# A streaming encoder layer on one Trainium2 core: a tile's final sum kept in PSUM, and the router's logits computed in two column halves

## What is computed

```python
def route(h, w_router, router_bias):
    scores = jax.nn.sigmoid(jnp.matmul(h, w_router, preferred_element_type=jnp.float32))   # (1088, 64)
    biased = scores + router_bias.astype(jnp.float32)
    ...                                      # best 4 of 8 groups, best 8 experts in them, their weights

    ffn = swiglu(hf, w_sh_gate, w_sh_up, w_sh_down) + routed_experts(hf, top_idx, top_w, ...)
    x = x + g2 * ffn.reshape(b, t, d)
...
y_prompt = rms_norm(yp) * final_gain
y_sample = rms_norm(ys) * final_gain
```

## Time and profile before

| | us |
|---|---|
| median of 3 runs | 2242.13 (2235.76 to 2243.9) |
| the profiled execution | 2241.32 |
| its span | 2239.5 |
| `mix_and_route`, mix of tile 0 to the last logits | 1017.8 to 1157.0 |
| closing part, from PE's last expert matmul | 2162.8 to 2239.5 |
| PE busy | 2141.2 (96%) |
| DVE busy | 1237.4 (55%) |
| ACT busy | 1008.1 (45%) |
| POOL busy | 463.4 (21%) |

### The profile page before, as it was taken

How to read it: one execution, slowest core, us unless ns; L and a number is a source line. 1 busy time by engine, 2 the same in 40 slices (tenths; PEclk the granted TensorE clock), 3 DMA queues, 4 the chain that set the end, 5 groups by cost and what they waited for, 6 DMA issues and landing times. The chain is left out here.

```text
span 2239.5 us, 41417 instructions
## 1 busy us (share of the span) xinstructions
PE 2141.2 (96%) x11538; PEld 1835.2 (82%) x11539; DVE 1237.4 (55%) x2000; ACT 1008.1 (45%) x1773; POOL 463.4 (21%) x549
## 2 busy tenths in 40 slices
PE   5999899999999999999988999999999999999995
PEld 3767559999999999997868888888888888888862
DVE  3623683112232332216777787687677778668637
ACT  3403793211111121113432677677677677667622
POOL 2400000000000000000000444434443444434344
PEclk8999899999999999999998999999999999999998
DMA  7370501112111101116312999899889899989876
GB/s 295 113 254 9 177 1 57 38 47 66 48 47 44 31 19 47 47 66 230 116 55 87 309 318 321 248 314 328 269 289 340 279 322 306 318 250 322 261 220 157
DMA packets 153532, 395.59 MB, mean 177 GB/s; under 512 B 22124, under 2 KB 90932, under 8 KB 128900
## 3 DMA queue, kind: packets, MB, share of 16 engines
q1 hardware_dynamic: 122260, 311.61, 38.5%
q0 software_dynamic: 31040, 82.51, 15.1%
q10 hardware_dynamic: 176, 0.75, 0.1%
HBM read 353.93 MB, written 74.53 MB: 191 GB/s over the span
## 5 line engine op out<-in xcount | busy, mean ns | idle before, releaser
L2093 PE MATMUL ex_pgu<-ex_wgu_hi,ex_xT_hi 128*128 (+1 forms) x784 | 314.9, 402 | 9.5 <-DVE ex_xT_lo L2263 8.7
L2251 DVE TENSOR_TENSOR ex_wgu_lo<-ex_stage_gu,ex_wgu_hi (+1 forms) x252 | 291.8, 1220 | 37.3 <-ACT ex_wgu_hi L2170 37.3
L2093 PE MATMUL ex_pgu<-ex_wgu_hi,ex_xT_lo 128*128 (+1 forms) x784 | 308.0, 393 | 0.0
L2093 PE MATMUL ex_pgu<-ex_wgu_lo,ex_xT_hi 128*128 (+1 forms) x784 | 307.1, 392 | 0.0
L2170 ACT CAST ex_wgu_hi<-ex_stage_gu (+1 forms) x252 | 245.7, 1047 | 35.6 <-issue 16.3
L986 PE MATMUL cv_ph<-fourth_r,cv_split 128*128 128x352 f32 (+1 forms) x1152 | 221.8, 327 | 0.8 <-ACT cv_split L997 0.8
L986 PEld LDWEIGHTS cv_ph<-fourth_r,cv_split 128*128 128x128 f32 x1152 | 195.8, 188 | 1.0 <-ACT cv_split L997 1.0
L1627 POOL MEMSET ex_rows<- 128x1088 f32 x1 | 1.0, 1005 | 944.3 <-ACT third_r L1599 944.3
L2093 PEld LDWEIGHTS ex_pgu<-ex_wgu_hi,ex_xT_hi 128*128 128x128 f32 x784 | 148.4, 189 | 41.4 <-issue 11.5
L2093 PEld LDWEIGHTS ex_pgu<-ex_wgu_hi,ex_xT_lo 128*128 128x128 f32 x784 | 147.5, 188 | 31.4
L2093 PEld LDWEIGHTS ex_pgu<-ex_wgu_lo,ex_xT_hi 128*128 128x128 f32 x784 | 147.9, 189 | 28.6
(11 more groups left out here) (355 smaller groups left out, 4197.0 us busy)
## 6 DMA issues: line engine op xcount, KB each, us to landing
ex_stage_gu<-in_w_exp_gate SPq DMA_DIRECT2D x64, 1024.0 KB, 9.0
ex_stage_gu<-in_w_exp_up SPq DMA_DIRECT2D x64, 1024.0 KB, 11.6
ex_stage_dn<-in_w_exp_down SPq DMA_DIRECT2D x64, 1024.0 KB, 8.6
front_room<-in_w_ada SPq DMA_DIRECT2D x26, 512.0 KB, 5.9
w_ahead<-in_w_in SPq DMA_DIRECT2D x24, 512.0 KB, 3.8
third<-in_w_ada SPq DMA_DIRECT2D x16, 512.0 KB, 8.8
early_late<-in_w_in SPq DMA_DIRECT2D x16, 512.0 KB, 3.9
front_room<-in_w_in SPq DMA_DIRECT2D x3, 2048.0 KB, 12.5
```

The lines of the kernel that those rows point to most:

```text
L2093: last = pe.matmul(pgu[:, :], xT[a][:, k, :], w, start=(k == 0 and (a, c) == PASSES[0]), stop=(k == KT - 1 and (a, c) == PASSES[-1]))
L2251: dve.tensor_tensor(gu_piece(1, slot, q), gu_raw(slot, q), gu_piece(0, slot, q).bitcast(F32), ALU.subtract).then_inc(gu_lo, 1)
```

## The change

1. Closing part. The addition of a tile writes into its PSUM pair, no longer into `sums[t]`. Square (ACT) and the scaled output (DVE) read that pair. For this the banks are also declared as four pairs of 1024 columns (`x3_rows`), and the order in which banks are handed out is changed so that each pair lies side by side. PE's wait before it uses a pair again is now on `o_ready` (output t-4 made) in place of `x3` (addition t-4 done).
2. Router logits. The eight matmuls have 64 columns of `wr` stationary and the tile's up to 128 tokens moving; the first four blocks of the contraction go to PSUM partitions 0 to 63, the last four to 64 to 127, by turns. ACT copies this 128 x 128 result to SBUF (`halves_out`), at the beginning of its next round, and a matmul with a fixed 128 x 64 matrix (two identities, one above the other, `both_halves`, made once by DVE) adds the halves and brings them to the old place (`sum_halves`). It stands six rounds into `mix` of tile t+3, and for the last tiles behind `logits(7)` and four matmul records into `unit(0)` and `unit(1)`.

```diff
@@ mix_and_route
+            both_halves = room(NE)
+            halves = [room(P), little(P)]
...
+                            if (k, pw, px) == ROUNDS[5] and t >= 3:
+                                sum_halves(t - 3)
...
-                        for k in range(KT):
-                            last = pe.matmul(pl[t % 2][:R, 0:NE], h2T[:, k, t * P:t * P + R], wr[:, k, :],
-                                             start=(k == 0), stop=(k == KT - 1))
-                        last.then_inc(lg, 1)
+                        for k in range(KT // 2):
+                            for a in range(2):
+                                j = a * (KT // 2) + k
+                                last = pe.matmul(pl[t % 2][a * NE:(a + 1) * NE, P:P + R], wr[:, j, :], h2T[:, j, t * P:t * P + R],
+                                                 start=(k == 0), stop=(k == KT // 2 - 1))
+                        last.then_inc(lg_halves, 1)
+
+                    def sum_halves(t):
+
+                        R = rows_of(t)
+                        pe.wait_ge(sum_ready, 1)
+                        pe.wait_ge(lg_out, t + 1)
+                        pe.matmul(pl[t % 2][:R, 0:NE], halves[t % 2][:, 0:R], both_halves, start=True, stop=True).then_inc(lg, 1)
...
+                                if half == 0 and k == 1 and q < 2:
+                                    sum_halves(NT - 2 + q)
...
                     logits(NT - 2)
+                    sum_halves(NT - 3)
                     unit(0)
...
+                    def halves_out(t):
+                        R = rows_of(t)
+                        act.wait_ge(lg_halves, t + 1)
+                        act.copy(halves[t % 2][:, 0:R], pl[t % 2][:, P:P + R]).then_inc(lg_out, 1)
...
                     for t in range(NT):
                         R = rows_of(t)
+                        if t >= 2:
+                            halves_out(t - 2)
                         act.wait_ge(x2_done, t + 1)
...
+                    halves_out(NT - 2)
                     sigmoid(NT - 2)
...
                     evac(NT - 1)
+                    halves_out(NT - 1)
                     sigmoid(NT - 1)
...
+                    dve.tensor_tensor(both_halves, con[:, C_ID:C_ID + NE], con[:, C_ID + NE:C_ID + P], ALU.add).then_inc(sum_ready, 1)
@@ experts
+            with ExitStack() as pairs:
+                x3_rows = [pairs.enter_context(nc.psum_tensor(f"cb_x3_{i}", [P, D], F32)) for i in range(4)]
             pt = [ps(f"ex_pt{i}", [P, 4, P]) for i in range(2)]
             pgu = ps("ex_pgu", [P, 2 * DE])
+            ph_bank = ps("ex_ph", [P, 512])
+            for j in range(2):
+                ps(f"cb_p{j}", [P, 512])
             py = [ps(f"ex_py{j}", [P, 512]) for j in range(2)]
-            ph_bank = ps("ex_ph", [P, 512])
...
-            ptail = [ps(f"cb_p{j}", [P, 512]) for j in range(2)]
...
+            psum = [[v[:, j * 512:(j + 1) * 512] for j in range(2)] for v in x3_rows]
...
                         if t >= 4:
-                            pe.wait_ge(x3, t - 3)
+                            pe.wait_ge(o_ready, t - 3)
...
-                        link(act.activation(junk[:R, :], sums[t][:R, :], ACT.Square, accum_out=ss[:R, t:t + 1]))
+                        link(act.activation(junk[:R, :], x3_rows[t % 4][:R, :], ACT.Square, accum_out=ss[:R, t:t + 1]))
...
-                        dve.scalar_tensor_tensor(out_rows[:R, t % 3, :], sums[t][:R, :], ri[:R, t:t + 1], gain[:R, :],
+                        dve.scalar_tensor_tensor(out_rows[:R, t % 3, :], x3_rows[t % 4][:R, :], ri[:R, t:t + 1], gain[:R, :],
                                                  ALU.mult, ALU.mult).then_inc(o_ready, 1)
...
                         for j in range(2):
-                            last = dve.tensor_tensor(v[:, j * 512:(j + 1) * 512], v[:, j * 512:(j + 1) * 512], psum[t % 4][j][:R, :], ALU.add)
+                            last = dve.tensor_tensor(psum[t % 4][j][:R, :], v[:, j * 512:(j + 1) * 512], psum[t % 4][j][:R, :], ALU.add)
                         last.then_inc(x3, 1)
```

More of the change, by code:

```diff
@@ L1261, in mix_and_route @@
         sh_down_loaded = S("sh_w_down")
+        lg_halves, lg_out, sum_ready = map(S, ("mx_logit_halves", "mx_logit_halves_out", "mx_sum_of_halves"))
         sh_loaded, sh_prod, sh_sig, sh_gated, sh_done = map(S, ("sh_w", "sh_prod", "sh_sig", "sh_gated", "sh_done"))
@@ L1880, in experts @@
             landed = sb("ex_landed", [1, 2])
+            with ExitStack() as pairs:
+                x3_rows = [pairs.enter_context(nc.psum_tensor(f"cb_x3_{i}", [P, D], F32)) for i in range(4)]
             pt = [ps(f"ex_pt{i}", [P, 4, P]) for i in range(2)]
             pgu = ps("ex_pgu", [P, 2 * DE])
+            ph_bank = ps("ex_ph", [P, 512])
+            for j in range(2):
+                ps(f"cb_p{j}", [P, 512])
             py = [ps(f"ex_py{j}", [P, 512]) for j in range(2)]
-            ph_bank = ps("ex_ph", [P, 512])
             ph = ph_bank[:, 0:NF * P].rearrange("p (f n) -> p f n", f=NF)
-            ptail = [ps(f"cb_p{j}", [P, 512]) for j in range(2)]
-            psum = [[v[:, :, :].rearrange("p a n -> p (a n)") for v in pt]] + [[v[:, :] for v in pair] for pair in ((pgu, ph_bank), ptail, py)]
+            psum = [[v[:, j * 512:(j + 1) * 512] for j in range(2)] for v in x3_rows]
             raw_gu = stage_gu[:, :, :].rearrange("p s n -> p (s n)")
```

## The result

The changed kernel takes 2232.05 us (median of 10 runs, 2230.01 to 2235.14), the kernel before, in the same rounds, 2241.99 (10 runs, 2235.76 to 2245.16): a ratio of 0.9956, 95% interval 0.9946 to 0.9966, or 9.9 us less. 2231.0 had been forecast. The profiled execution took 2230.64 us, its span is 2228.8. The lines of the changed kernel: mix L1444, transposes L1456, logits L1469, `sum_halves` L1478, `unit` L1487, counts L1531; the last sums L2158 and L2162, POOL's multiplication L2100, reciprocal L2348, scaled output L2351, addition L2365, Square L2271.

The account below looks back on a forecast made before the run. PE, busy for 96% of the span, was taken as the bound. Closing part -9.0 us and router -2.0 made -11.0, from the median of 2242.13 to 2231.1, predicted as 2231; range 2225 to 2239.

Parts of the forecast that it names:

- The stall: Closing part: POOL's multiplications keep out tile 0's scaled output, with two SBUF inputs; 19.38 us becomes 1.28 with one in PSUM.
- What is late next: Closing part: PE's tile 4 now waits for output 0, behind addition 1, and begins at 2194.95, 4.6 us worse.
- PE's five tiles in one go: Closing part: later outputs are ready before PE asks, so PE runs its last five tiles without a gap, 26.05 us.
- The clock's loss: Closing part: after some 7 us idle PE restarts at a lower clock and loses 1.7 us, bounds 0 and 3.
- The write into PSUM: Closing part: an addition that writes to PSUM in place costs DVE nothing more; upper bound twice the time.
- The rival of +2.6: Closing part: additions in place in PSUM are slow, +2.6 us, total 2233.7; chance 8%.
- The round: Mix stage, per tile: logits 1.2 us for 1.7, summing the column halves +0.2, net -0.3; 13.3 us in all.
- The end of the stage: Mix stage after mix 8: shorter logits 7 and 8 against the last sums of halves, together -0.2 us.
- The cover for sigmoid 6: End of mix stage: sigmoid 6 comes 1.2 to 2.5 us later; DVE's 2.49 us wait covers it, or half a microsecond short.
- Halves in turn: Router logits: the column halves don't overlap, +0.55 us a tile, +4.3 in all, total 2237.4; chance 10%.
- Full gain: Router logits: changes of tile form cost nothing, logits 0.86 us a tile, router -4.3, total 2228.8; chance 9%.
- The stall stays: Closing part: one SBUF input is enough to keep the scaled output out; +7.1 us, total 2249; chance 5%.

Follow-up runs that it names:

- e3_no_gate: The kernel before without POOL's nine multiplications of the tile sums by the gate: 2228.85 us, one run.
- e4_pool_pauses: The kernel before, but from tile 3 on POOL's gate multiplication of tile t waits until output t-3 is made: 2228.68 us, ratio 0.9932 to before.
- e5_in_turn: The changed kernel, but a tile's logit matmuls go first all to the lower column half, then all to the upper: 2236.84 us, one run.

## Why the prediction held, step by step

- *The stall* was what I took it for. That a PSUM input lets the scaled output in rested on one addition beside POOL; nine outputs of 1.28 us, and e3_no_gate and e4_pool_pauses from the other side, bear it out.
- *What is late next* was right to the hundredth: tile 4 waits for output 0 and starts 8.39 us after POOL's first multiplication (forecast 2194.95 - 2186.56 = 8.39, measured 2192.00 - 2183.61). This wait is the dearest part of the new order: e4_pool_pauses avoids it and the loss of clock behind it, 4.6 and 2.8 us.
- *PE's five tiles in one go* were 26.05; measured 2221.05 - 2192.00 = 29.05, all of the 3.0 above it in the first tile. What follows PE was 7.8 and is 2228.8 - 2221.05 = 7.75.
- *The clock's loss* is the mis-sized term: 1.7 taken, 3.0 measured, the upper bound. It is all that parts the forecast of -9.0 from the measured -7.7. I had read its size off a single restart; five more (table) give 1.6 to 2.2 by the same reckoning, so that 3.0, at my upper bound, is the largest of the seven restarts with a loss. Against the 3.67 of a restart at full clock it is 2.8.
- *The write into PSUM* at nothing: 1.29 for two, as I took it. The rival of +2.6 falls.
- *The round*: -0.3 a tile forecast, -0.30 measured, but from terms that err against each other. The logits take 1.03 and 0.09 (forecast 1.2), the sum of the halves adds 0.28 to a mix (0.2). My reading that 107 ns is what moving 128 fp32 columns costs doesn't stand: in e5_in_turn such records take 94.
- *The end of the stage*: -0.2 forecast (my own terms, -0.5, +0.2, +0.2 and -0.2, add up to -0.3), and this step failed by 0.8 us: from logits 7 to the counts it is 21.65 us and was 22.69, 1.04 less. The rounds before it give 1.89 and not 1.8. Logits 7 give 1.42 (1.0 forecast), logits 8 give 0.45 (0.2), the three sums cost 0.49, 0.32 and 0.26, near the forecast; the last 0.24 is in the units between. The cover for sigmoid 6 was enough: at the counts DVE still waits 1.10 us for PE (2.49 before). So the router gives 2.9 in its stage, not 2.0.
- The two errors, 1.3 too much and 0.9 too little, nearly cancel. That the total is right to 1 us (2232.05 against 2231.0) is partly luck.
- *Halves in turn*, the rival of most weight, had its price wrong. e5_in_turn shows it at +0.2 us for the stage (146.94 against 146.74), where I had +4.3: its premise, 107 ns whatever the form, did not hold. *Full gain* falls with 1.03 against 0.86.
- *The stall stays*: nothing of it was seen. Nor does POOL get in the way: its last two multiplications waited 0.89 us for a DMA, while PE had three tiles in front of it.

## What to carry to other kernels

In this kernel a DVE instruction with two large SBUF inputs that stood beside an uninterrupted row of POOL multiplications cost the rest of that row, and not its own length. Look for such a pair, and move one input to PSUM, or let POOL wait once in a while: the second is a smaller edit and was worth more here by the stretches (39.4 against 44.4), because the first made a buffer come free later. When a stall goes, look at what the freed buffer's next user waits for, and at how long PE stands still in front of it: sixteen records of filler, issued into a pause, were worth 2.6 us here.

## What the runs showed that I had not expected

- The loss behind a pause of PE did not grow with the pause: after 13.35 us the first eight records took 5.13 and 5.61, after 6.5 to 7 us 5.06, 5.60 and 6.44, after 4.95 and after 2.45 5.37. After 1.54, 1.81, 1.99 and 2.20 us they took 3.67. Whether 2.45 against 2.20 us is what decided, and what makes the loss 1.6 or 3.0, no run shows.
- POOL's multiplications kept the scaled output waiting over seven of them in a row (tiles 2 to 8, 19.38 us), with DMA starts in between, while an addition with one SBUF input went through beside them.
- With 64 columns of weights and 128 moving, an fp32 record takes 94 ns in turn and 64 by turns, and 107 with 128 and 64; the difference between 107 and 94 is unexplained.
